# 64-row head matmuls, half-height query tiles and six raw weight slots in a two-block attention network

## The reference

```python
h = _rmsnorm(x, norm_g)
p = _split_columns(h @ w_in)
y_a = _dsa_attention(q_a, k_a, v_a, qi, ki, p['idx_w'])      # top-k of 4 index heads of 32, then softmax
y_b = _fox_attention(heads(p['fox_q']), heads(p['fox_k']), heads(p['fox_v']), log_f)   # softmax with decay
y_c = _stick_breaking_attention(heads(p['sb_q']), heads(p['sb_k']), heads(p['sb_v']))
y_d = _nsa_attention(q_d, ...)                               # compressed, selected and window keys
y_e = _memory_attention(heads(p['mem_q']), mem_k, mem_v)     # 256 memory rows
merge = jax.nn.sigmoid(p['merge'].reshape(B, S, N_BRANCH, D_MODEL))
merged = jnp.sum(merge * jnp.einsum('bsnc,ncd->bsnd', ys, w_branch), axis=2)
return x + merged @ w_out
```

## Time and profile before

| | |
|---|---|
| median of three runs | 4074.5 us (4072.53 to 4077.92) |
| the profiled execution | 4069.02 us |
| its span in the trace | 4067.7 us |
| granted TensorE clock, mean | 0.943 |
| TensorE (PE) busy | 3623.6 us (89%), 17198 instructions |
| weight loads (PEld) | 2755.1 us (68%) |
| VectorE (DVE) busy | 1745.5 us (43%) |
| ScalarE (ACT) busy | 1271.0 us (31%) |
| GpSimd (POOL) busy | 931.5 us (23%) |

### The profile page before, as it was taken

One profiled execution on the slowest core, in us unless ns is written; L12 is line 12 of the kernel. 1 busy time (PEld: TensorE's weight loads), 2 busy tenths in 40 slices (PEclk: granted clock), 3 DMA queues, 4 the chain that ended last, 5 costly groups with the idle time before them and its releaser, 6 DMA issues. The chain is left out here.

```text
span 4067.7 us, 44507 instructions
## 1 busy us (share of the span) xinstructions
PE 3623.6 (89%) x17198; PEld 2755.1 (68%) x17198; DVE 1745.5 (43%) x3310; ACT 1271.0 (31%) x2122; POOL 931.5 (23%) x415
## 2 busy tenths in 40 slices
PE   6998999989898898989968787899998888998998
PEld 4644777767654577767656556788886646876877
DVE  3227334433223733533379652522354375534233
ACT  2332323332332232333231342322233224533332
POOL 2111221113311222212322201222363100023443
PEclk9999898999999999989978898999999799999999
DMA  3342112123333211212211101121242010012222
GB/s 116 121 130 83 54 63 63 61 79 102 105 124 119 88 45 65 65 50 97 89 46 57 47 1 42 42 68 63 69 139 78 17 57 1 1 47 73 94 93 78
DMA packets 86467, 288.08 MB, mean 71 GB/s; under 512 B 9840, under 2 KB 20592, under 8 KB 85232
## 3 DMA queue, kind: packets, MB, share of 16 engines
q1 hardware_dynamic: 85248, 275.41, 20.8%
q10 hardware_dynamic: 1008, 9.83, 0.7%
HBM read 281.01 MB, written 4.19 MB: 70 GB/s over the span
## 5 line engine op out<-in xcount | busy, mean ns | idle before, releaser
L378 POOL TENSOR_TENSOR weights_low<-weights_loaded,weights_high 128x1024 fp32r<-128x1024 f32 (+2 forms) x377 | 899.2, 2385 | 2877.0 <-ACT weights_high L360 2648.5
L291 PE MATMUL psum<-h_high,weights_high 128*128 128x512 f32 (+1 forms) x2384 | 918.5, 385 | 66.8 <-DVE h_low L515 26.2
L292 PE MATMUL psum<-h_low,weights_high 128*128 128x512 f32 (+1 forms) x2384 | 890.4, 373 | 0.0
L293 PE MATMUL psum<-h_high,weights_low 128*128 128x512 f32 (+1 forms) x2384 | 888.2, 373 | 0.0
L360 ACT CAST weights_high<-weights_loaded 128x1024 fp32r<-128x1024 f32 (+2 forms) x377 | 391.9, 1040 | 608.5 <-PE psum L293 503.8
L291 PEld LDWEIGHTS psum<-h_high,weights_high 128*128 128x128 f32 x2384 | 459.3, 193 | 167.1 <-issue 73.2
L292 PEld LDWEIGHTS psum<-h_low,weights_high 128*128 128x128 f32 x2384 | 459.5, 193 | 86.6 <-issue 11.1
L293 PEld LDWEIGHTS psum<-h_high,weights_low 128*128 128x128 f32 x2384 | 458.1, 192 | 79.4
L3175 DVE TENSOR_TENSOR act_low<-ffn_act,act_high 128x512 fp32r<-128x512 f32 (+1 forms) x66 | 141.2, 2140 | 142.7 <-ACT act_high L3154 142.5
L291 PE MATMUL psum<-act_high,weights_high 128*128 128x512 f32 (+1 forms) x528 | 189.8, 359 | 10.0 <-DVE act_low L3175 10.0
L291 PE MATMUL psum<-weights_high,h_high 128*128 128x512 f32 (+4 forms) x480 | 162.2, 338 | 40.6 <-ACT mixed_features L2161 21.6
(11 more groups left out here) (374 smaller groups left out, 5326.8 us busy)
## 6 DMA issues: line engine op xcount, KB each, us to landing
weights_loaded<-stream_dram SPq DMA_DIRECT2D x480, 512.0 KB, 3.4
weights_loaded<-stream_dram SPq DMA_DIRECT2D x81, 128.0 KB, 2.8
weights_loaded<-stream_dram SPq DMA_DIRECT2D x12, 384.0 KB, 3.3
weights_loaded<-stream_dram SPq DMA_DIRECT2D x8, 272.0 KB, 2.9
x<-x_dram SPq DMA_DIRECT2D x1, 2048.0 KB, 9.8
arena_mem<-mem_dram ACTq DMA_DIRECT2D x2, 1024.0 KB, 5.9
x<-x_dram ACTq DMA_DIRECT2D x1, 2048.0 KB, 7.9
x_kept_dram<-x ACTq DMA_DIRECT2D x1, 2048.0 KB, 6.5
```

The costliest lines, as they stand in the source:

```text
L291: pe.matmul(out, a.high, b.high, start=start, stop=False)
L292: pe.matmul(out, a.high, b.low, start=False, stop=False)
L293: return pe.matmul(out, a.low, b.high, start=False, stop=stop)
L378: pool.tensor_tensor(self.low[s][:, 0:size], raw[:, 0:size], self.high[s][:, 0:size], ALU.subtract).then_inc(*g.event("weights_low").up(po ...
```

## The change

- The query tiles of sb, dsa, fox, nsa and mem, and `ml_q`, are half as large: [128, 2, n]. A head's matmul takes the 64 rows on which it lies (`half_of`), of queries and keys alike.
- No half is cleared any more: `padded_gpsimd` and `first_gpsimd` go, and with them the event "zeroed" and what the branches waited for it.
- A pair of heads is drained, roped or copied by one operation over 128 partitions.
- fox has two `fa` tiles in place of four; the order of heads on the 32-row groups is [0, 2, 1, 3], and constants, bias and projection columns follow it.
- NRAW is 6 in place of 4; the arenas shrink (30, 33 and 24 times 256 columns to 26, 29 and 20), and the norm's scratch tiles of the second block share memory in another way.

```diff
-NRAW = 4
+NRAW = 6
...
-def head_halves(out):
-
-    if isinstance(out, tuple):
-        return [(slice(HD * i, HD * (i + 1)), o) for i, o in enumerate(out)]
-    return [(slice(0, P), out)]
-
-
 def pair_scalar(g, key, out, scale=1.0):
     act = g.act
-    for part, o in head_halves(out):
-        for m in g.after(act, g.event("projected").at(key)):
-            act.wait_ge(*m)
-        act.activation(o, g.bank(key)[part, :], ACT.Copy, scale=scale).then_inc(
-            *g.event("drained").up(act, key))
+    for m in g.after(act, g.event("projected").at(key)):
+        act.wait_ge(*m)
+    act.activation(out, g.bank(key), ACT.Copy, scale=scale).then_inc(*g.event("drained").up(act, key))
 
 
 def pair_vector(g, key, out, scale=1.0):
     dve = g.dve
-    for part, o in head_halves(out):
-        for m in g.after(dve, g.event("projected").at(key)):
-            dve.wait_ge(*m)
-        dve.tensor_scalar(o, g.bank(key)[part, :], scale, None, ALU.mult).then_inc(
-            *g.event("drained").up(dve, key))
+    for m in g.after(dve, g.event("projected").at(key)):
+        dve.wait_ge(*m)
+    dve.tensor_scalar(out, g.bank(key), scale, None, ALU.mult).then_inc(*g.event("drained").up(dve, key))
+
+
+def half_of(h):
+
+    return slice(HD * (h % 2), HD * (h % 2 + 1))
...
-    for part, o in head_halves(out):
-        for m in g.after(dve):
-            dve.wait_ge(*m)
-        dve.tensor_tensor(o, tmp[part, :], raw[part, :], ALU.add).then_inc(*S("roped").up(dve, key))
+    for m in g.after(dve):
+        dve.wait_ge(*m)
+    dve.tensor_tensor(out, tmp[:, :], raw[:, :], ALU.add).then_inc(*S("roped").up(dve, key))
...
-        out, kt, at = g.banks(i)[:, 0:u.keys], keys_of(u, h), slice(u.qt * P, (u.qt + 1) * P)
+        out, rows, at = g.banks(i)[:, 0:u.keys], half_of(h), slice(u.qt * P, (u.qt + 1) * P)
         for m in g.after(pe, *ready):
             pe.wait_ge(*m)
-        done = mm(g, out, q[:, h, at], kt, True, extra is None)
+        done = mm(g, out, q[rows, h // 2, at], keys_of(u, h)[rows, :], True, extra is None)
         if extra is not None:
-            done = mm(g, out, extra[0][:, h, at], extra[1][:, 0:u.keys], False, True)
+            done = mm(g, out, extra[0][rows, h // 2, at], extra[1][rows, 0:u.keys], False, True)
...
-def padded_gpsimd(g, key, q):
-    pool, S = g.pool, g.event
-    pairs = q.rearrange("p (j g) n -> p j g n", g=2)
-    for i in range(2):
-        for m in g.after(pool):
-            pool.wait_ge(*m)
-        pool.memset(pairs[HD * (1 - i):HD * (2 - i), :, i, :], 0.0).then_inc(
-            *S("zeroed").up(pool, key if i else None))
...
+FOX_SLOTS = [0, 2, 1, 3]
...
-    for h in range(HEADS):
+    for j in range(2):
         for m in g.after(dve):
             dve.wait_ge(*m)
-        dve.tensor_scalar(t.fa[:, h, :], t.g[:, :], g.c.fox[:, 2 * h:2 * h + 1],
-                          g.c.fox[:, 2 * h + 1:2 * h + 2], ALU.mult, ALU.add).then_inc(*S("decay").up(dve))
...
-    ready = [S("zeroed").at(("sb", l)), S("drained").at(key("v"))]
+    ready = [S("drained").at(key("v"))]
...
-        j = hd // 2
+        j, rows = hd // 2, half_of(hd)
         for b in range(QT):
             i = g.claim(key("z", hd, b), turn.next(1))
             for m in g.after(pe, *ready):
                 pe.wait_ge(*m)
-            mm(g, g.banks(i)[:, 0:SEQ - b * P], t.k[:, j, b * P:(b + 1) * P], t.q[:, hd, b * P:SEQ], True,
+            mm(g, g.banks(i)[:, 0:SEQ - b * P], t.k[rows, j, b * P:(b + 1) * P], t.q[rows, j, b * P:SEQ], True,
                True).then_inc(*S("scored").up(pe, key(hd, b)))
         fill_tensor(g)
         for b in range(QT):
             n = SEQ - b * P
             bank = g.banks(g.claim(key("w", hd, b), turn.next(1)))
-            mm(g, bank[:, 0:n], t.k[:, j, b * P:(b + 1) * P], t.q[:, hd, b * P:SEQ], True, False)
+            mm(g, bank[:, 0:n], t.k[rows, j, b * P:(b + 1) * P], t.q[rows, j, b * P:SEQ], True, False)
...
-def first_gpsimd(g):
-    pool, t = g.pool, g.t
-    tiles = {2: t.sb, 0: t.dsa, 1: t.fox, 3: t.nsa}
-    for l in range(DEPTH):
-        for i, b in enumerate(BRANCH_ORDER):
-            name = BRANCH_NAME[b]
-            g.weights.low_parts((name, l))
-            for m in g.after(pool, *(g.all_at(("closed", l, i - 2)) if i > 1 else g.all_at(("gates", l)))):
-                pool.wait_ge(*m)
-            padded_gpsimd(g, (name, l), tiles[b].q)
-        g.weights.low_parts(("mem", l))
-        for m in g.after(pool, *g.all_at(("closed", l, 3))):
-            pool.wait_ge(*m)
-        padded_gpsimd(g, ("mem", l), t.mem.q)
 
 
...
         if name == "q":
-            for i in range(2):
-                half = slice(ML_QK * i, ML_QK * (i + 1))
-                for m in g.after(act, S("projected").at(k), S("zeroed").at("ml_q")):
-                    act.wait_ge(*m)
-                act.copy(t.ml_q[half, 2 * j + i, :], g.wide(k)[half, :]).then_inc(*S("drained").up(act, k))
+            copy_scalar(g, k, t.ml_q[:, j, :], g.wide(k))
...
-    for name, tile, value in (("ml_q", t.ml_q[:, :, :], 0.0), ("up", t.up[:, :, :], 0.0),
+    for name, tile, value in (("up", t.up[:, :, :], 0.0),
...
+        rows = half_of(h)
...
-                        done = mm(g, g.wide(k, x0, x1), t.ml_k[:, h // 2, kb * P:(kb + 1) * P], t.ml_q[:, h, x0:x1],
-                                  True, True)
+                        done = mm(g, g.wide(k, x0, x1), t.ml_k[rows, h // 2, kb * P:(kb + 1) * P],
+                                  t.ml_q[rows, h // 2, x0:x1], True, True)
...
-            even, odd = sb("arena_even", [P, 30 * 256], s2), sb("arena_odd", [P, 33 * 256], s2)
+            even, odd = sb("arena_even", [P, 26 * 256], s2), sb("arena_odd", [P, 29 * 256], s2)
...
-    heads = [("q", [P, HEADS, SEQ]), ("k", [P, 2, SEQ]), ("v", [P, QT, BR])]
+    heads = [("q", [P, 2, SEQ]), ("k", [P, 2, SEQ]), ("v", [P, QT, BR])]
```

More of the change, by code:

```diff
@@ L1162, in finish_plain_vector @@
     return finish
-def pair_of(q, j):
-    return tuple(q[HD * i:HD * (i + 1), 2 * j + i, :] for i in range(2))
 def paired(k):
@@ L1247, in dsa_tensor @@
                 fill_tensor(g)
-    ready = [S("zeroed").at(("dsa", l)), S("drained").at(key("v"))]
+    ready = [S("drained").at(key("v"))]
     ready += [S("roped").at(key(n, j)) for n in "qk" for j in range(2)]
@@ L1341, in fox_tensor @@
     key = lambda *a: ("fox", l) + a
[L1342 removed]
+    project(g, key("f"), turn, np.repeat(COL["fox_f"][FOX_SLOTS], 32), (l,), h)
     for j in range(2):
@@ L1346, in fox_tensor @@
     values_tensor(g, key("v"), turn, COL["fox_v"], (l,), h)
-    ready = [S("zeroed").at(("fox", l)), S("drained").at(key("v")), S("decay").at(l)]
+    ready = [S("drained").at(key("v")), S("decay").at(l)]
     ready += [S("drained").at(key(n, j)) for n in "qk" for j in range(2)]
@@ L1595, in nsa_tensor @@
         g.weights.used(c, "projected", key("wc2", which))
-    ready = [S("zeroed").at(("nsa", l)), S("drained").at(key("v")), S("drained").at(key("wc2", "k")),
+    ready = [S("drained").at(key("v")), S("drained").at(key("wc2", "k")),
              S("drained").at(key("wc2", "v"))]
@@ L1695, in mem_tensor @@
     values_tensor(g, key("v"), turn, BR + np.arange(BR), (l,), t.mem, ntile=nt, name="w_mem_kv")
-    ready = [S("zeroed").at(("mem", l)), S("drained").at(key("v"))]
+    ready = [S("drained").at(key("v"))]
     ready += [S("drained").at(key(n, j)) for n in "qk" for j in range(2)]
@@ L1771 @@
 BRANCH_ORDER = (2, 0, 1, 3)
-BRANCH_NAME = {0: "dsa", 1: "fox", 2: "sb", 3: "nsa"}
 FIRST_FILL, FIRST_MAIN = (6, 2), (0, 6)
```

51 lines of the change are left out of this document (27 added, 24 removed).

## The result

The changed kernel takes 4120.45 us by the median of four runs (4115.85 to 4123.15); the kernel before, beside it, 4076.21 us. The ratio is 1.0108, with a 95% interval of [1.0091, 1.0126]: 44 us slower, where 9 were forecast and 4101 was the upper end. The profiled execution took 4123.15 us with a granted clock of 0.935 (0.943 before).

What follows compares the result with a forecast made beforehand. TensorE, busy 3623.6 of 4067.7 us, was taken as the bound. Stream +20.2, ring -7.8 and output projection -3.5 summed to +8.9; against the 4074.5 median that gave 4083.4 us, range 4058 to 4101.

Steps and rivals of the forecast that it cites:

- A seam is 0.20, in or out: TensorE's stream: each uncovered change between 64 and 128 rows costs 0.20 us; 246 seams, +49.2 us.
- the first rival (0.10 a seam): TensorE's stream: a seam costs only the drain, 0.10 us, giving 4059 us; chance 0.18.
- A pair takes the time of one head: Softmax logits: two adjacent head matmuls on opposite halves take the time of one; -29.0 us in all.
- the "no pairs" rival: Softmax logits: two 64-row heads go one after the other, +29 us, 4112 us; chance 0.08.
- The softmax branches' sum: Logits, per layer: dsa +0.8, fox -0.6, nsa +2.0, mem +1.8 us; +8.0 in all.
- The mLSTM: +1.6, from eight seams: mLSTM: a new seam between scores and read for 8 pairs of direction and head, +1.6 us.
- The layout of the arenas moves addresses only: Tiles' places in memory: the new arena layout changes addresses only, priced at nothing.
- The ring, -11.3: Six raw slots let weight chunks come earlier: -7.8 us over both layers, net -3.5 at the output projection.
- the stretch of the keys: ACT's mla_k copies: two casts of 1.05 us stand in front, in a stretch that DVE bounds, +1.8 us.
- Cleared halves, drains and decay rows at nothing: POOL's clears, ACT's and DVE's drains, fox's decay rows: nothing lost, at most 2 x 3 us gained.
- Every 64-row load exposed, 4123: Rival, TensorE's stream: about 374 of 704 instructions pay a 0.107 us weight load, +40 us, 4123 us; chance 0.03.
- The sign (slower): Whole kernel: slower than before, beyond the "same" band of 4066.4 to 4082.6 us; chance 0.50.

Runs made afterwards that it cites:

- b_off8: The kernel before with eight unused columns among the first block's constants, moving h and the tiles behind it by 32 bytes: 4091.22 against 4073.81 us.
- a_pad: The changed kernel with four unused columns among the first block's constants: 4090.81 us, against 4077.14 for the kernel before.
- a_ml128: The changed kernel with 128-row mLSTM scores, four unused columns among the first block's constants and five raw slots: 4072.08 us, against 4073.81 for the kernel before.
- b_sb: The kernel before with only the z and w matmuls of sb taking the head's 64 rows: 4089.15 against 4077.54 us.
- b_ml_even: The kernel before with 64-row mLSTM scores for heads 0 and 2 only, 128 rows for heads 1 and 3: 4087.55 against 4077.12 us.
- b_ring5_x64: The kernel before with five raw slots and unused columns so that nearly all tiles start at multiples of 64 bytes: 4073.01 against 4073.81 us.
- b_soft: The kernel before with 64-row logits in dsa, fox, nsa and mem alone: 4081.70 against 4077.14 us.

## Why the prediction was wrong, point by point

By the differences of medians, each against the kernel before beside it: sb +11.6, softmax branches +4.6, mLSTM +22.0, place +17.4 (b_off8), six slots for four -14.7. The sum is +40.9 of the measured +44.2; the rest is within the intervals. The place is the least certain of them: taken from a_pad it is +31, and the sum would be 54.

- *A seam is 0.20, in or out*: right. sb, all seams and no pairs, gave 11.6 for 10.8 (11.4 by the stages of its trace). So the first rival (0.10 a seam) falls.
- *A pair takes the time of one head*: right, read off the timeline; with it the "no pairs" rival falls. The softmax branches' sum was 8.0 and measured 4.6, with an interval that holds both.
- *The mLSTM: +1.6, from eight seams*: this is the step that failed most. It priced the edit by the seams alone and took the granted clock of the stage as given. It measured +22.0: with 64-row scores TensorE falls back to the lower of its two levels (1.2 for 2.4 GHz) again and again, in the scores and in the ml_v matmuls behind them. The earlier trace rows held a warning, a stage with TensorE idle for 31 of 142 us and a clock of 0.90 (in the 100 us of the scores, 14 idle at 0.94 and 0.98), next to stages at 1.00. It was no proof. sb and fox, where TensorE has little idle time, kept 0.99 and 1.00 with 64 rows, and dsa, with its few 64-row logits, kept its 0.94 though idle for 18 of 90 us. An estimate from the steps (0.43 us for 512 columns) says how much they differ in another respect too: 64-row matmuls are some 17 of sb's 116 us, but some 5 of the 13 us of a round in the mLSTM. Which of the two, waits or share, decides was not tested.
- *"The layout of the arenas moves addresses only", priced at nothing*: failed, +17.4 by b_off8 (31 by a_pad). That h had moved by 32 bytes against a multiple of 64 was to be seen in the programs and was not looked for.
- *The ring, -11.3*: right in kind and in place: the waits of 1.84 and 1.40 for POOL are gone in both layers, and that of 5.60. The size, -14.7 measured, is near, but stage by stage it came otherwise: the 150 us behind sb are 3.0 us shorter in layer 0 and 0.9 in layer 1 (3.9 forecast for each), the 35 us from 3605 on 7.6 shorter (5.2), and the stretch of the keys 1.8 longer, as forecast. (5.2 less 1.8 is 3.4; the prediction has 3.5.)
- *Cleared halves, drains and decay rows at nothing*: nothing speaks against it; a_ml128, which has none of them in the first block, adds up without a term for them. They were not tried alone.
- *Every 64-row load exposed, 4123*: this rival's time came out to within 3 us and its mechanism is wrong. The second of two 64-row instructions starts 0.43 after the first, with its load hidden, and the sb stages of b_sb are 11.4 us longer where it asks for 17. A right number was no evidence for the mechanism; only the runs by parts told.
- The sign (slower) was right, with a chance of 0.50, and that was in good part luck: of the terms that the prediction did price well, sb, the softmax branches and the ring, the measured sum is +1.5 us. Slower came from the clock and from the place in memory, neither of which was in its sum.

## What to carry to other kernels

Halving the rows of a matmul costs nothing in the stream and gives a second head on the other half for free, but each change of rows costs 0.2 us here, so halves pay only where two of them stand next to each other. And they can cost a stage its clock. The one that lost it here had both waits of TensorE and a large share of 64-row work; look at the granted clock before, and try such a stage alone. An edit that resizes a tile moves those behind it: compare start addresses of the matmuls' tiles in both programs before pricing it at nothing. And when a change bundles a gain (slots) with losses (rows), run the gain alone.

## What the runs showed of the hardware

- In the mLSTM the granted clock depends on how many rows the scores take, at unchanged count and columns: 0.98 with 128-row scores, 0.78 with 64-row ones (second halves), and ml_v is back at 4.85 us within a round when the scores take 128 rows again (b_ml_even). The rows that the kernel before takes in addition are multiplied by zeros, so the products that aren't zero are the same in both: rows count here even when they hold zeros. Which mixes of rows and waits bring the fall was not settled; sb and fox kept their clock.
- 512-column fp32r matmuls step by 227 or 233 ns by where h starts (a_pad, b_off8). Which places are good was not settled: with nearly all tiles at multiples of 64, five groups of matmuls stepped faster and those of the feed-forward nets more slowly (b_ring5_x64).
- In the first feed-forward net, 256-column matmuls stepped by 113 ns in one profiled execution (before) and by 118 in others with its tiles in the same places (b_sb, b_soft), 5 us over 330. Neither edit touches that net, so it looks like scatter from execution to execution, and may be part of why the kernel before ranged from 4060 to 4086 us; no second trace of that kernel is there to show it.
